# One product for the softmax denominators, and the v_s bias as a row of the matmul group instead of an add on VectorE

## What is computed

```python
h = rmsnorm(x); proj = h @ w_in + b_in              # (S, 2816)
q, k, v, z_a, u_s, v_s, z_s = split(proj)           # 512,128,128,512,512,512,512
# mixer A: window of 128, 8 query heads, 2 kv heads, blocks of 128 queries
p = exp(scores) * mask                              # keys of the block before and of the block itself
attn = (p @ v) / (sum(p) + exp(sink)) * silu(z_a)
# mixer B: per chunk of 128 positions
v_s = layernorm(gelu(v_s)); mixed = W_s(lower triangle) @ v_s + b_s
sgu = gelu(u_s) * mixed * silu(z_s)
out = rmsnorm(x + [attn, sgu] @ w_out + b_out)
```

## Time and profile before

| | us |
|---|---|
| median of 3 runs | 571.77 (571.29 to 572.77) |
| the profiled execution | 572.77 |
| its span on the slowest core (core 7), first to last instruction | 571.2 |
| PE, DVE, ACT, POOL busy in that span | 509.7, 356.5, 338.9, 257.4 |

### The profile page before, as it was taken

The page is one execution under the profiler, slowest core; times in us unless marked ns, Lnnn a source line. Parts: engine busy times, 40 slices in busy tenths (PEclk is TensorE's granted clock), DMA queues, the critical chain, the costliest instruction groups (busy, mean ns, idle before and its releaser), DMA issues.

```text
span 571.2 us, 9533 instructions; the slowest of 8 cores (566.9 to 571.2 us)
## 1 busy us (share of the span) xinstructions
PE 509.7 (89%) x3106; PEld 236.5 (41%) x3106; DVE 356.5 (62%) x458; ACT 338.9 (59%) x576; POOL 257.4 (45%) x283
## 2 busy tenths in 40 slices
PE   1898699999997989999899989999899989999961
PEld 1365244443443435343354444443354444443420
DVE  2766597575767593567637685475736486375763
ACT  4235765757684756558577574748568476347531
POOL 2013598271367164441536356361454537171572
PEclk9999979999999999999999999999999999999987
DMA  7999990520233042503404043221512023100351
GB/s 226 324 338 310 317 185 8 149 75 0 111 112 110 39 148 73 175 12 93 165 38 149 1 149 110 111 76 38 179 42 74 2 102 120 73 2 19 129 218 76
DMA packets 19200, 66.85 MB, mean 117 GB/s; under 512 B 2256, under 2 KB 2384, under 8 KB 19152
## 3 DMA queue, kind: packets, MB, share of 16 engines
q1 hardware_dynamic: 17856, 64.11, 33.6%
q0 software_dynamic: 1152, 2.10, 2.4%
q10 hardware_dynamic: 144, 0.05, 0.1%
HBM read 51.56 MB, written 16.78 MB: 120 GB/s over the span
## 4 chain that ended last, share of the span: by engine, by line
PE 64%; issue 12%; DVE 9%; ACT 6%; POOL 5%; DMA 2%; POOLq 0%; DVEq 0%; SPq 0%; ACTq 0%
PE pp L498 32%; PE pp L702 14%; PE pp L552 4%; PE pp L655 3%; PE pp L523 3%; PE pp L628 2%; PE pp L659 2%; DMA xa<-x 2%; ACT LR L668 2%; PE pp L598 2%; DVE xe L707 1%; DVE vs_f L557 1%; PE pp L537 1%; PE pp L482 1%; POOL LR L674 1%
## 5 line engine op out<-in xcount | busy, mean ns | idle before, releaser
L498 PE MATMUL pp<-xT,w_fm 128*128 128x512 bf16 x1088 | 245.7, 382 | 7.2 <-DVE xe L707 2.0
L498 PEld LDWEIGHTS pp<-xT,w_fm 128*128 128x128 bf16 x1088 | 104.5, 98 | 139.5 <-issue 20.1
L702 PE MATMUL pp<-w_out_bf,mixT 128*128 128x512 bf16 x512 | 121.8, 383 | 9.4 <-DVE mixT L678 6.4
L688 POOL TENSOR_TENSOR xe<-xe,bout_sb 128x1024 f32<-128x1024 f32 x32 | 80.9, 2532 | 14.7 <-DMA xe<-x 14.6
L702 PEld LDWEIGHTS pp<-w_out_bf,mixT 128*128 128x128 bf16 x512 | 46.3, 98 | 72.3 <-issue 26.3
L674 POOL TENSOR_TENSOR LR<-LR,zaT 128x512 f32<-128x512 f32 x32 | 40.9, 1278 | 75.9 <-ACT LR L672 75.8
L707 DVE TENSOR_TENSOR xe<-pp,xe 128x512 f32<-128x512 f32 x64 | 43.6, 687 | 49.7 <-PE pp L702 46.3
L633 ACT ACTIVATE PT<-pp 128x1024 bf16<-128x1024 f32 x63 | 62.7, 1030 | 6.2 <-PE pp L628 6.2
L716 DVE SCALAR_TENSOR_TENSOR xe<-xe,st_fr,gf_sb 128x1024 f32<-128x1024 f32 x32 | 48.7, 1522 | 27.1 <-POOL st_fr L714 26.7
L646 DVE TENSOR_TENSOR PT<-PT,pack_b_sb 128x1024 bf16<-128x1024 bf16 x58 | 54.0, 940 | 6.7 <-ACT PT L633 5.7
L668 ACT ACTIVATE LR<-pp,esink 128x128 f32<-128x128 f32 x128 | 36.4, 367 | 35.3 <-PE pp L659 35.2
(11 more groups left out here) (60 smaller groups left out, 593.5 us busy)
## 6 DMA issues: line engine op xcount, KB each, us to landing
xa<-x SPq DMA_DIRECT2D x32, 512.0 KB, 6.4
xe<-x SPq DMA_DIRECT2D x32, 512.0 KB, 3.8
out<-xe SPq DMA_DIRECT2D x32, 512.0 KB, 2.7
xe<-w_in SPq DMA_DIRECT2D x12, 512.0 KB, 12.4
mixT<-w_in SPq DMA_DIRECT2D x10, 512.0 KB, 14.7
w_out_bf<-w_out POOLq DMA_DIRECT2D x8, 256.0 KB, 9.4
LR<-sgu_wT SPq DMA_DIRECT2D x1, 512.0 KB, 17.0
bout_sb<-bout_bc SPq DMA_DIRECT2D x1, 512.0 KB, 18.3
```

What stands on the lines that cost most here:

```text
L498: ins = e.matmul(bank(h), lhsT=w_fm[:, FM.index(cb), k, :], rhs=xT[:, xb, k, :], start=(k == 0), stop=(k == 7))
L688: G.op("pool", lambda e: e.tensor_tensor(out=xe[:, s, :], in0=xe[:, s, :], in1=bout[:], op=ALU.add), reads=["c_bout"], writes=[("xe", s, 0 ...
L702: ins = e.matmul(bank(h), lhsT=mixT[:, mb, ec, tt * 128:(tt + 1) * 128], rhs=w_out[:, ec, hf * 512:(hf + 1) * 512], start=(ec == 0), stop= ...
```

## The change

Two things are exchanged between PE and DVE.

1. The denominators. DVE adds the two masked key blocks of `PT` into a new tile `PC` (31 blocks; block 0 has only one key block). PE then makes one matmul with the ones per kv head, on `PC`, where it made two. `mmpv` waits for `PC` as well.
2. The bias of v_s. Each v_s group gets a ninth matmul that ends it: one row of ones (`ones_row`, one partition) against the bias as one row (`bvs_row`). DVE's add is gone; ACT applies Gelu from PSUM to `vs_f`, and that frees the bank. The v_s matmuls get a gate, so that they are planned only when their Gelu phase has come. `vs_f` has two slots, not three.

Beside that: the bias comes in as [1, 512] (2 KB) into a part of `sgt` and DVE copies it to bf16, in place of a load of [128, 512] (256 KB); POOL sets `ones_row`; costs are rewritten (v_s tile 1.73 to 2.1, quarter of stage 0 1.8 to 2.6, `mmpv` 0.95 to 0.72), from which the planner makes a new order for all engines.

```diff
-    bvs_d = din("bvs_bc", [128, 512])
+    bvs_d = din("bvs_row", [1, 512])
...
-        vs_f = sb("vs_f", [128, 3, 512], F32)
+        vs_f = sb("vs_f", [128, 2, 512], F32)
...
+        PC = sb("PC", [128, 2, 1024], BF16)
+        ones_row = sb("ones_row", [1, 128], BF16)
-        bvs = sb("bvs_sb", [128, 512], F32)
+        bvs_row = sb("bvs_row_sb", [1, 512], BF16)
...
+        G.op("pool", lambda e: e.memset(ones_row[:], 1.0), writes=["ones_row"], prio=-9)
...
                 def mmvs(e, c=c):
                     for tt in range(4):
                         for k in range(8):
-                            ins = e.matmul(bank(hs[tt])[:, c * 128:(c + 1) * 128], lhsT=xT[:, 0, k, tt * 128:(tt + 1) * 128],
-                                           rhs=w_vs[:, k, c * 128:(c + 1) * 128], start=(k == 0), stop=(k == 7))
+                            e.matmul(bank(hs[tt])[:, c * 128:(c + 1) * 128], lhsT=xT[:, 0, k, tt * 128:(tt + 1) * 128],
+                                     rhs=w_vs[:, k, c * 128:(c + 1) * 128], start=(k == 0), stop=False)
+                        ins = e.matmul(bank(hs[tt])[:, c * 128:(c + 1) * 128], lhsT=ones_row[0:1, :],
+                                       rhs=bvs_row[0:1, c * 128:(c + 1) * 128], start=False, stop=True)
                     return ins
-                G.op("pe", mmvs, reads=[("xT", 0, t) for t in range(4)] + [("w", CB_VS + c)],
-                     writes=[("vs0", t) for t in range(4)], cost=1.8, alloc=hs if c == 0 else (),
-                     uses=() if c == 0 else hs, prio=-0.38 + 0.02 * c, mode="full")
+                G.op("pe", mmvs, reads=[("xT", 0, t) for t in range(4)] + [("w", CB_VS + c), "ones_row", "bvs_row"],
+                     writes=[("vs0", t) for t in range(4)], cost=2.6, alloc=hs if c == 0 else (),
+                     uses=() if c == 0 else hs, prio=-0.38 + 0.02 * c, mode="full", gate=PH_GELU)
...
-            xb, vb = st % 2, (4 * st + tt) % 3
+            xb, vb = st % 2, tt % 2
...
                 def mmvs(e):
                     for k in range(8):
-                        ins = e.matmul(bank(h), lhsT=xT[:, xb, k, tt * 128:(tt + 1) * 128], rhs=w_vs[:, k, :], start=(k == 0),
-                                       stop=(k == 7))
-                    return ins
-                G.op("pe", mmvs, reads=[("xT", xb, tt)] + [("w", CB_VS + c) for c in range(4)], cost=1.73,
-                     alloc=[h], prio=v0, mode="full")
-            G.op("dve", lambda e: e.tensor_tensor(out=vs_f[:, vb, :], in0=bank(h), in1=bvs[:], op=ALU.add), uses=[h],
-                 reads=([("vs0", tt)] if st == 0 else []) + ["c_bvs"], writes=[("vs_f", vb)], cost=0.68, prio=v0 - 0.3)
-            G.op("act", lambda e: e.activation(out=vs_f[:, vb, :], in_=vs_f[:, vb, :], func=AF.Gelu), writes=[("vs_f", vb)],
-                 cost=0.6, prio=v0 - 0.3, phase=3 * st + PH_GELU)
+                        e.matmul(bank(h), lhsT=xT[:, xb, k, tt * 128:(tt + 1) * 128], rhs=w_vs[:, k, :], start=(k == 0), stop=False)
+                    return e.matmul(bank(h), lhsT=ones_row[0:1, :], rhs=bvs_row[0:1, :], start=False, stop=True)
+                G.op("pe", mmvs, reads=[("xT", xb, tt), "ones_row", "bvs_row"] + [("w", CB_VS + c) for c in range(4)], cost=2.1,
+                     alloc=[h], prio=v0, mode="full", gate=3 * st + PH_GELU)
+            G.op("act", lambda e: e.activation(out=vs_f[:, vb, :], in_=bank(h), func=AF.Gelu), uses=[h],
+                 reads=[("vs0", tt)] if st == 0 else [], writes=[("vs_f", vb)], cost=0.6, prio=v0 - 0.3, phase=3 * st + PH_GELU)
...
                 for g in range(2):
-                    for i, kb in enumerate(kbs):
-                        ins = e.matmul(bank(hd)[g * 64:(g + 1) * 64, :], lhsT=ones64[:, :], rhs=PT[:, p2, kb, g * 512:(g + 1) * 512],
-                                       start=(i == 0), stop=(i == len(kbs) - 1))
+                    ins = e.matmul(bank(hd)[g * 64:(g + 1) * 64, :], lhsT=ones64[:, :],
+                                   rhs=(PC[:, p2, :] if n else PT[:, p2, 1, :])[:, g * 512:(g + 1) * 512], start=True, stop=True)
                 return ins
-            G.op("pe", mmpv, reads=[("PT", p2, kb) for kb in kbs] + [("v", (n - 1 + kb) // 4 % 3) for kb in kbs] + ["ones64"],
-                 cost=0.95, alloc=[hn, hd], prio=v0 - 11, mode="col")
+            if n:
+
+                G.op("dve", lambda e: e.tensor_tensor(out=PC[:, p2, :], in0=PT[:, p2, 0, :], in1=PT[:, p2, 1, :], op=ALU.add),
+                     reads=[("PT", p2, 0), ("PT", p2, 1)], writes=[("PC", p2)], cost=0.66, prio=v0 - 0.5)
+            G.op("pe", mmpv, reads=[("PT", p2, kb) for kb in kbs] + [("v", (n - 1 + kb) // 4 % 3) for kb in kbs] + ["ones64"]
+                 + ([("PC", p2)] if n else []), cost=0.72, alloc=[hn, hd], prio=v0 - 11, mode="col")
...
-            load_const("c_bvs", bvs[:], bvs_d, eng="sp", kb=256, prio=-1.4 + 0.125)
+            bvs_f = sgt[0:1, 1, :]
+            load_const([("sgt", 1)], bvs_f, bvs_d, eng="sp", kb=2, prio=-1.4 + 0.025)
...
+            G.op("dve", lambda e: e.tensor_copy(out=bvs_row[:], in_=bvs_f), reads=[("sgt", 1)], writes=["bvs_row"], cost=0.4, prio=-0.9)
```

More of the change, by code:

```diff
@@ L818, in _host_layout @@
         "w_out": w_out[rows, :],
-        "bvs_bc": np.broadcast_to(b_p[CB_VS:CB_VS + 4].reshape(1, 512), (128, 512)),
+        "bvs_row": b_p[CB_VS:CB_VS + 4].reshape(1, 512),
         "sgu_wT": np.asarray(inp["sgu_w"])[0].transpose(2, 0, 1),
```

## The result

The changed kernel takes 586.7 us (586.33 and 587.04), 1.026 times the kernel before, 95% interval 1.023 to 1.030: 15 us slower. The profiled execution took 587.04 us with a span of 585.5 us on core 2, 14.3 us longer than before.

What follows compares the result with a forecast made beforehand. PE was taken as the bound, busy 446.2 of 468.0 us from 72 to 540 us. Terms -6.8 + 12.0 + 2.2 + 2.3 - 3.3 + 2.6 = +9.0 on 572.8 gave 581.8, median 1.0 lower: 580.8 us, range 569.5 to 590.

Steps and rivals of the forecast that it cites:

- The case that I took for the likeliest: Whole kernel: slower, at 576 to 588 us; chance 0.50.
- Denominators on PE, -6.8: mmpv on PE: one matmul pair of 0.22 us fewer in 31 blocks, -6.8 us, bounds -6.8 and 0.
- Bias rows, +12.0: v_s on PE, stages 1 to 7: a ninth, one-row matmul in 28 tiles at 0.43 us each, +12.0 us; other end 6.0.
- The first rival: v_s bias rows: a row costs no more than its columns, 6.0 us plus 1.7 in stage 0, giving 573.1 us; chance 0.20.
- Stage-0 rows, +2.2: Stage 0 on PE: sixteen bias rows cost 4.3 us, half swallowed by waits, +2.2 us; ends 0 and 4.3.
- DVE's adds, +2.3: Exp phases: 31 adds, 21.4 to 29.1 us of DVE, make PE wait at a rate of 8%, +2.3 us; ends 0 and 29.1.
- The v_s chain, -3.3: Gelu phases: PE's waits of 2.5 and 0.8 us around DVE's v_s eviction go, -3.3 us; ends 0 and -11.9.
- The gate, +2.6: Stage 1's Exp phase: three early v_s tiles, 5.2 us, move to the Gelu phase; half lost, +2.6 us; ends 0 and 12.1.
- The rest: nothing: Start of the kernel: smaller bias load, one DVE copy and one POOL memset cost nothing, under 0.7 us without room on DVE.
- My sign that stages below 66 us would disprove the sum: Stages: the prediction is wrong if they shrink below 66 us although PE's busy time rises by some 9 us.
- DVE as the bound: Exp phases: mmpv waits for masks and adds; 608 us if every add holds up PE, 593 if every second; chance 0.12.
- The faster rival: Gelu phases: all 11.9 us of PE's v_s chain waits go and the gate costs nothing, giving 569.6 us; chance 0.18.

Runs made afterwards that it cites:

- e5: e2 with the old four denominator matmuls per block back on PE; DVE's add stays, its result unused: 567.4 us.
- e2: The kernel before with the first part of the change alone (denominators through PC), v_s bias still added by DVE, no gate: 563.4 us, ratio 0.987.
- e4: The changed kernel in its own order, with the bias row and the ones as full products of 128 rows, stage 0 included: 578.2 us, ratio 1.012.
- e11: The kernel before's operations, old products and no PC add, in the order planned for e2 (engine choices included): 558.6 us, ratio 0.977.
- e6: e2 with the PC add cut to 32 of 1024 columns and unused; denominators from the current key block alone: 555.9 us, one execution.
- e9: The changed kernel in its own order, with POOL's first four bout adds moved behind the fourth LR product of the first stage: 580.3 us, ratio 1.016.
- e7: e2 with the gate on the v_s matmuls, bias still added by DVE: longest span 568.6 us, against 561.8 in e2.
- e8: The changed kernel without the gate on the v_s matmuls, in stage 0 as well: 582.1 us, ratio 1.018.

## Why the prediction was right, and where not

I forecast 580.8 us, slower, in a range of 569.5 to 590; it is 586.7. The case that I took for the likeliest came. But single terms were off by as much as the miss of 6 or by twice as much, the new order one way, the adds on DVE and the jam the other. That they nearly cancelled is luck.

- **Denominators on PE, -6.8.** An `mmpv` with three pairs takes 0.78 us, 0.77 forecast (151.87 to 152.65). Taken alone, its effect is -4.0 us (e5 to e2). The pair is 0.22 us of PE; a part of it went into waits, as the bound of 0 allowed.
- **Bias rows, +12.0.** This step held: 0.41 us from tile to tile above the 1.73 of eight alone, 0.43 forecast; four rows in a middle stage come to 1.64 us, and the whole change's stage is 1.70 us longer than e2's. The nearest row, a matmul of 64 rows between full ones, was the right one to go by. The first rival (573.1) needed the row to cost 0.22, and that is what a row of 128 costs (e4). The Trainium skill's sentence that 32 rows take the same time as 128 (TensorE: Matmul & The Clock Gate, "Why this matters for your kernels") holds for the length of the record and not for the distance. Another of its pages fits: TensorEngine Tiling (Array Packing), "Key Properties", says that changing the tiling mode drains TensorE; it gives no time, the rows here give 0.2 us there and back; whether a matmul of one row is such a change of mode, no run shows.
- **Stage-0 rows, +2.2 (0 to 4.3).** The groups take 11.35 us after (38.59 to 49.94) for 7.15 before: +4.2. With full rows they take 8.04, 3.3 less, and the first load comes 2.8 us earlier (e4; 2.3 in the mean of the eight cores), so most of it shows.
- **DVE's adds, +2.3 (0 to 29.1).** Undersized. The adds by themselves cost 8.8 us (e11 to e5), 7.5 when thinned out (e6): 0.5 us per middle stage, some 3.5 us over seven, not far from what the 8% rate gives, and 3.4 (e6) to 7.3 us (e11 to e5) in the first stage, where that rate does not hold; POOL's bout adds run beside them there. Their busy time came out above my upper bound: mean 1.418 us, 44.0 us in all. 12.56 us of that are the one in the jam, and the other thirty come to 31.4, above the bound of 29.1 too. I had taken the mask's worst case of 2.85 us for the worst that contention does. (The 23.5 us of waits that I took the rate from leave out a row of 2.0 us for `sgt`; with it the term would be 2.5.)

```profile
L665 DVE TENSOR_TENSOR PC<-PT 128x1024 bf16<-128x1024 bf16 x31 | 44.0, 1418 | 0.1
```

- **The jam in the first stage: no step of mine.** 6.4 us by e9, and more by its cores. It is contention of the kind that I named, at a size that I did not.
- **The v_s chain, -3.3.** The waits for `st_mv` and `vs_f` are gone, and Gelu from PSUM is no slower (597 ns for 629). But they are gone in e11 too, where the add is still on DVE: the new order is enough to end them, and that the missing link did is not shown. Per middle stage the whole change is 1.46 us above e7, where four rows cost 1.64: some 0.2 us per stage is left for it at most. What is won ahead of the first Exp load (65.6 for 68.1 in e7, in spite of the stage-0 rows) can't be told apart from the smaller load and another order.
- **The gate, +2.6 (0 to 12.1).** +6.8 by e7, with a jam in it, and 4.6 by e8. The mechanism is the one named, work held back from a stretch with idle time into a full one. I took half of the 5.2 us of three tiles; the row of a full Exp phase spoke for all of it, and after the change the second and the third Exp load are just 5.2 us further apart than before.
- **"The rest: nothing", and a fixed order.** This is the largest error. A new set of costs means a new order everywhere, and that of the first change was worth -12.9 us to the old operations (e11). I had priced the operations as if each kept its place and its engine. What the old operations take in the order of the whole change was not run. My sign that stages below 66 us would disprove the sum came true (64.9): the sum was near in PE's busy time (+10.3, forecast 9.5, though some of the 10.3 is the lower clock behind the jam) and wrong about the waits. Those behind line 678 (683 after) did not rise above 7.1 us but fell to 3.3 and 2.4 at two places, though DVE had more to do.
- **DVE as the bound** did not happen in the steady state (42.7 of 64.9 us busy). **The faster rival** failed: from 145 us on the 6.4 us of waits behind the v_s chain did end, but the longest one, in stage 0, stayed (6.2 us after), and the gate's price did not shrink with them.

The terms as measured: order -12.9, adds +8.8, products -4.0, gate +6.8, rows +11.9 (seven stages of 1.70) and some 2.8 in stage 0, jam +6.4 make +19.8; the change is +15.2. This is no full account: the first three were measured in e2's order and not in that of the whole change, the gate's term has a jam in it that the last term may count again, and the 4.6 us between hold the v_s chain and the start too. No run separates them.

## What to carry to other kernels

Where a planner orders the work, a change of its costs is a change of the whole order, and of the engines where it may choose them: before a gain or loss is put down to an edit, run the old operations in the new order. A product of a single row between full ones should be padded to the full shape if the zeros are free. Before an operation with two SBUF inputs is given to VectorE, look at what GpSimd does in the same stretch, and move there what can come later.

## What the runs showed of the hardware

- **A DVE instruction can be passed over by a whole run of POOL instructions.** It concerned instructions with both inputs in SBUF (mask, gating product, `PC` add): 12.56 us after, 8.9 in e8, 7.15 in e7, 5.9 in e9, each for an instruction of some 0.7 us; where I compared them (after, e7, e9) it ended 0.55 us after POOL's last one. The eviction from PSUM that started at 78.27, beside the same POOL run, kept its 0.74 us. The Trainium skill (SBUF — State Buffer, "Who interferes with whom") has an instruction with two SBUF inputs contend with a GpSimd instruction that reads SBUF, for ports that are an exclusive lock. A wait for one GpSimd instruction fits that, as the 2.83 us beside a single bout add in e2; a wait for seven is more than it says. In e2 POOL was as busy from 81 to 93 us, and DVE got its turn after each instruction (DVE, then POOL). What decides between the two stays open.

```profile
81.40 2.83 DVE L611 TENSOR_TENSOR mixT<-sgt,uT 128x512 bf16<-128x512 f32 x1
...
80.89 5.56 POOL L692 TENSOR_TENSOR xe<-xe,bout_sb 128x1024 f32<-128x1024 f32 x2
86.41 1.60 POOL L678 TENSOR_TENSOR LR<-LR,zaT 128x512 f32<-128x512 f32 x1
87.98 5.54 POOL L692 TENSOR_TENSOR xe<-xe,bout_sb 128x1024 f32<-128x1024 f32 x2
```

- **One row costs more than 128.** A matmul of 512 columns with one row between full ones takes 0.41 us of PE's time, with 128 rows 0.22.
